# Splitting a head's query and key norm over ScalarE, VectorE and GpSimd

## What is computed

```python
def rms_norm(x, g):
    xf = x.astype(F32)
    xf = xf * lax.rsqrt(jnp.mean(xf * xf, axis=-1, keepdims=True) + EPS)
    return (xf * g.astype(F32)).astype(x.dtype)

    # in mixer_ab (layer 0)
    q = rms_norm(q.reshape(b_, t, B_KV_HEADS, B_GROUP, B_HEAD_DIM), q_g)
    k = rms_norm(k.reshape(b_, t, B_KV_HEADS, B_HEAD_DIM), k_g)
    ...
        qr = rope_2d(q, row, col)
        k_all = jnp.concatenate([rope_2d(k, row, col), ctx_k], axis=1)
    y_b = gqa_attend(qr, k_all, v_all).reshape(b_, t, B_WIDTH) * jax.nn.silu(g_b)
```

## Time and profile before

| | us |
|---|---|
| median of 3 runs (lowest, highest) | 2848.95 (2845.6, 2851.0) |
| the profiled execution, device time | 2847.76 |
| its span, first to last instruction | 2846.2 |
| PE busy | 2586.5 (91%) |
| DVE busy | 1776.5 (62%) |
| ACT busy | 867.0 (30%) |
| POOL busy | 426.9 (15%) |

### The profile page before, as it was taken

One profiled execution on the slowest core, in us unless ns is written; L12 is line 12 of the kernel. 1 busy time (PEld: TensorE's weight loads), 2 busy tenths in 40 slices (PEclk: granted clock), 3 DMA queues, 4 the chain that ended last, 5 costly groups with the idle time before them and its releaser, 6 DMA issues.

```text
span 2846.2 us, 38995 instructions
## 1 busy us (share of the span) xinstructions
PE 2586.5 (91%) x12050; PEld 2050.7 (72%) x12050; DVE 1776.5 (62%) x3260; ACT 867.0 (30%) x1767; POOL 426.9 (15%) x483
## 2 busy tenths in 40 slices
PE   4779999998888979979999999999999999988995
PEld 3458877787766858868877777777777777766884
DVE  4665777777778546766445555565656555554675
ACT  4532223232222222223223333333333333322221
POOL 0000211122221110000021212121222211001001
PEclk9789999999999989989999999999999999998998
DMA  7844544444433365553432222222222222236555
GB/s 251 294 157 148 183 135 146 158 151 161 155 127 124 131 239 190 177 192 129 155 99 91 84 67 90 91 90 88 74 90 90 92 93 90 88 112 214 181 192 213
DMA packets 167001, 400.72 MB, mean 141 GB/s; under 512 B 14984, under 2 KB 16656, under 8 KB 161616
## 3 DMA queue, kind: packets, MB, share of 16 engines
q1 hardware_dynamic: 133152, 249.08, 27.3%
q0 software_dynamic: 33712, 149.96, 15.0%
HBM read 338.17 MB, written 63.18 MB: 141 GB/s over the span
## 4 chain that ended last, share of the span: by engine, by line
PE 68%; DVE 14%; DVEq 6%; DMA 4%; issue 4%; ACT 2%; POOL 0%; SPq 0%; ACTq 0%; POOLq 0%
PE ps L533 53%; PE ps L420 5%; DVE w_lo L1072 3%; PE ps L411 3%; PE ps L429 3%; DMA w_raw<-in_w_ada_dram 2%; DVEq L1099 2%; ACT w_hi L720 1%; DVE small L954 1%; DVE work L971 1%; DMA stage<-z 1%; PE ps L512 1%; DVEq L1161 1%; PE ps L553 1%; DVE work L1181 1%
## 5 line engine op out<-in xcount | busy, mean ns | idle before, releaser
L533 PE MATMUL ps<-w_hi,hT_hi 128*128 128x512 f32 x2800 | 1163.9, 416 | 14.2 <-issue 7.5
L533 PE MATMUL ps<-w_hi,hT_lo 128*128 128x512 f32 x2800 | 1107.3, 395 | 0.0
L533 PE MATMUL ps<-w_lo,hT_hi 128*128 128x512 f32 x2800 | 1106.1, 395 | 0.0
L1072 DVE TENSOR_TENSOR w_lo<-w_raw,w_hi 128x512 fp32r<-128x512 f32 x688 | 490.2, 719 | 407.2 <-ACT w_hi L720 392.8
L533 PEld LDWEIGHTS ps<-w_hi,hT_hi 128*128 128x128 f32 x2800 | 535.1, 191 | 137.7 <-issue 37.8
L533 PEld LDWEIGHTS ps<-w_hi,hT_lo 128*128 128x128 f32 x2800 | 533.3, 190 | 118.9
L533 PEld LDWEIGHTS ps<-w_lo,hT_hi 128*128 128x128 f32 x2800 | 535.7, 191 | 91.7 <-issue 1.4
L720 ACT CAST w_hi<-w_raw 128x512 fp32r<-128x512 f32 x688 | 421.1, 620 | 506.4 <-PE ps L533 440.3
L1106 DVE SCALAR_TENSOR_TENSOR ada_sum<-w_raw,cond,ada_sum 128x512 f32<-128x512 f32 x480 | 366.8, 805 | 37.7 <-issue 10.8
L681 ACT ACTIVATE work<-ps,small 128x640 f32<-128x640 f32 (+1 forms) x192 | 139.0, 724 | 579.9 <-DVE small L957 579.8
L954 DVE TENSOR_REDUCE small<-ps 128x1 f32<-128x640 f32 (+1 forms) x200 | 143.7, 718 | 106.0 <-PE ps L420 96.4
(11 more groups left out here) (173 smaller groups left out, 2242.0 us busy)
## 6 DMA issues: line engine op xcount, KB each, us to landing
w_raw<-in_w_in_dram SPq DMA_DIRECT2D x216, 512.0 KB, 3.8
w_raw<-in_w_ada_dram SPq DMA_DIRECT2D x256, 256.0 KB, 3.0
z<-stage POOLq DMA_DIRECT2D x27, 1280.0 KB, 5.2
w_raw<-in_w_ada_dram SPq DMA_DIRECT2D x64, 512.0 KB, 5.1
w_raw<-in_w_out_dram SPq DMA_DIRECT2D x64, 512.0 KB, 4.2
work<-z POOLq DMA_DIRECT2D x72, 320.0 KB, 3.8
work<-in_x_sample_dram POOLq DMA_DIRECT2D x12, 1024.0 KB, 5.9
work<-o POOLq DMA_DIRECT2D x8, 1280.0 KB, 8.0
```

Of the source, the lines that this page charges most:

```text
L533: last = nc.tensor.matmul(ps[:, t, :], x[:, kt, t * P:(t + 1) * P], w[:, kt % RING, :], start=(kt == 0 and i == 0), stop=(kt == KT - 1 and ...
L1072: nc.vector.tensor_tensor(w_lo[:, kt % RING, :], w_raw[:, i % RAW, kt % 2, :], w_hi[:, kt % RING, :].bitcast(F32), ALU.subtract).then_inc( ...
```

## The change

Three engines share the norm of a layer 0 head, where DVE did it alone.

- **ACT**: a new `square_head` does the squares and their sums, with one `activation` of Square and `accum_out` for each of the ten 128x128 tiles of query and key. It writes the squares themselves into `weights`. The query's five stand behind the T step with r = 5 (slot 28 of pairs 0 to 3), the key's five behind the one with r = 6 (slot 43). For head 0 they stand behind k tiles 6 and 8 of chunk C_L0 + 2; the loop over two chunks there is written out for that.
- **DVE**: `norm_head` waits for `squared`, and makes the roots only, in four parts (`rsqrt_parts`) behind the same four first steps; it signals `rooted`. `before_pairs` isn't changed: the first part for head 0 stands beside k tile 4.
- **POOL**: `rotate_head` of layer 0 waits for `rooted`, and then does the four products of 128x640 with root and weight itself, with a drain behind each, ahead of the rotation.

```diff
@@ -249,7 +249,8 @@
                 s = lambda n: sem(f"{n}_{l}")
                 self.qk_in = s("qk_in")
                 self.v_in = s("v_in")
-                self.normed = s("head_normed")
+                self.squared = s("head_squared")
+                self.rooted = s("head_rooted")
                 self.roped = s("head_roped")
                 self.t_ready = s("t_ready")
                 self.t_hi = s("t_hi")
@@ -659,7 +660,22 @@
                 project_chunk(j + C_O1, j + 31, finish_at(72, j + 20, True))
 
 
-        def attention_act(act, L, h, order=None):
+        def square_head(act, h, parts):
+
+            s = S[0]
+            act.drain()
+            if 0 in parts:
+                act.wait_ge(s.qk_in, h * 48 + 48)
+                if not isinstance(h, int) or h > 0:
+                    act.wait_ge(s.rooted, h)
+            for n in parts:
+                for t in range(TT):
+                    last = nc.scalar.activation(weights[:, n, t * P:(t + 1) * P], (q_in, k_in)[n][:, t, :], ACT.Square,
+                                                accum_out=small[:, 40 + 5 * n + t:41 + 5 * n + t])
+            if 1 in parts:
+                last.then_inc(s.squared, 1)
+
+        def attention_act(act, L, h, order=None, last_head=False):
             s = S[L.n]
             NT, NS = L.n_turn, L.n_scores
 
@@ -697,6 +713,8 @@
                         nc.scalar.copy(vv[0][:, TT, :], cv_in[:, :]).then_inc(s.v_hi, 1)
                     turn(r, pieces[r])
                     r += 1
+                    if L.maps == 1 and not last_head and r in (6, 7):
+                        square_head(act, h + 1, (r - 6,))
                 elif kind == "S":
                     if n < TS * L.maps:
                         scores(n, n // L.maps, ps[:, SC:SC + 2, 0:320], 640)
@@ -806,12 +824,18 @@
                 feed_hi(0, kt)
             split_chunk(C_L0, feed_beside(0))
             evacuate(C_L0, 0)
-            with act.Fori(0, 2) as i:
-                split_chunk(i + (C_L0 + 1))
-                evacuate(i + (C_L0 + 1), i + 1)
+            split_chunk(C_L0 + 1)
+            evacuate(C_L0 + 1, 1)
+
+            def square_first(kt):
+                if kt == 6 or kt == 8:
+                    square_head(act, 0, (kt // 2 - 3,))
+
+            split_chunk(C_L0 + 2, square_first)
+            evacuate(C_L0 + 2, 2)
 
             def pair0(i, pace, evac, order=None):
-                steps = attention_act(act, L0, i, order)
+                steps = attention_act(act, L0, i, order, order is ORDER0T)
                 split_chunk(i + C_P0, stepper(steps, pace))
                 finish(steps)
                 evac(i + C_P0, i + 3)
@@ -887,28 +911,11 @@
 
             s = S[0]
             dve.drain()
-            dve.wait_ge(s.qk_in, h * 48 + 48)
-            for n, z in enumerate((q_in, k_in)):
-                if n == 1:
-                    dve.drain()
-                nc.vector.tensor_tensor(squares[0], z[:, :, :], z[:, :, :], ALU.mult)
-                dve.drain()
-                nc.vector.tensor_reduce(small[:, 40 + 5 * n:45 + 5 * n], squares[0], AX_X, ALU.add)
-                yield
-            dve.drain()
+            dve.wait_ge(s.squared, h + 1)
             nc.vector.tensor_scalar(small[:, 40:50], small[:, 40:50], 1.0 / P, EPS, ALU.mult, ALU.add)
             dve.drain()
-            rsqrt(dve, small[:, 40:50], small[:, 50:60], small[:, 30:40])
-            yield
-            for n, (z, g) in enumerate(((q_in, gq), (k_in, gk))):
-                nc.vector.tensor_tensor(z[:, :, :], z[:, :, :],
-                                        small[:, 50 + 5 * n:55 + 5 * n].unsqueeze(2).to_broadcast([P, TT, P]), ALU.mult)
-                dve.drain()
-                last = nc.vector.tensor_tensor(z[:, :, :], z[:, :, :], g[:, :].unsqueeze(1).to_broadcast([P, TT, P]),
-                                               ALU.mult)
-                if n == 0:
-                    yield
-            dve.drain().then_inc(s.normed, 1)
+            yield from rsqrt_parts(dve, small[:, 40:50], small[:, 50:60], small[:, 30:40])
+            dve.drain().then_inc(s.rooted, 1)
 
         def norm_out(dve):
 
@@ -1405,7 +1412,15 @@
 
                 s = S[L.n]
                 if L.n == 0:
-                    wait(s.normed, h + 1)
+                    wait(s.rooted, h + 1)
+                    for n, (z, g) in enumerate(((q_in, gq), (k_in, gk))):
+                        nc.gpsimd.tensor_tensor(z[:, :, :], z[:, :, :],
+                                                small[:, 50 + 5 * n:55 + 5 * n].unsqueeze(2).to_broadcast([P, TT, P]),
+                                                ALU.mult)
+                        pool.drain()
+                        nc.gpsimd.tensor_tensor(z[:, :, :], z[:, :, :],
+                                                g[:, :].unsqueeze(1).to_broadcast([P, TT, P]), ALU.mult)
+                        pool.drain()
                 else:
                     wait(s.qk_in, h * 48 + 48)
                 half = L.dk // 4
```

## The result

The changed kernel takes **2854.0 us** (median; 2846.5 to 2862.5), the kernel before in the same comparison 2845.6 (2842.6 to 2851.2). The ratio is 1.0027 with a 95% interval of 1.0017 to 1.0036: slower, by 5 to 10 us. The forecast was 2870 in a range of 2852 to 2890. The sign was right and the time lies just inside the range, but of the 21.6 us that the steps added up to, only 8 were there.

The account below looks back on a forecast made before the run. PE was taken to bound the kernel, held where it waits on other engines. Pairs 0 to 3 +4.8, pairs 4 to 6 +8.5 and head 0 +8.3 make 21.6 us on 2849.0: forecast 2870, range 2852 to 2890.

Parts of the forecast that it names:

- What bounds the kernel, and the places: PE bounds; its waits for L986 and at G steps go, new ones stand at the next pairs' first T.
- Head 0, +8.3: Near 326 us DVE waits for ACT's squares: PE stalls 5.9 us, plus 1.7 clock and 0.7 afterwards.
- ACT's squares, 0.1 us a pair: Ten squares with sums on ACT, five taking 1.8 us, delay PE by 0.1 us a pair, bound 0 to 1.
- the length of POOL's chain: From `rooted` to a pair's first T: products 8.4 us a head (2.1 each), then rotation 11.7, or 12.3 in pair 4.
- the seven transitions: Starts of pairs 1 to 7: +4.8 us for the first four and +8.5 for the last three.
- The clock: A low stretch costs 1.7 us: one lost, one added per transition in pairs 0 to 3; +5.1 in pairs 4 to 6.
- Pairs 0 to 3, forecast +4.8: Four transitions at +1.2 us net: first T +0.3, ada wait -0.8, clock +1.7; PE idles 5.3 us at the start.
- Pairs 4 to 6, forecast +8.5: Later first T from POOL's longer work, +2.6, +0.4 and +0.4 us, plus 5.1 of clock; bounds 0 and +18.
- The shared port, the second rival: POOL's longer work slows DVE's ada and w_lo, making DVE late: 2894 us, or 2886 at two thirds; chance 0.15.
- DVE's busy time: Over the whole kernel, DVE's busy time falls by some 45 us net of what contention adds.
- The third rival: Room is enough for half: products 1.6 to 1.7 us, no more low clock, head 0 costs 8; 2847 to 2854; chance 0.13.
- One more sum: POOL's products at 1.4 us each, by the skill's element count, would make the total 15 us lower.

Follow-up runs that it names:

- experiment 1: The changed kernel with head 0's squares on ACT two k tiles earlier and DVE's root parts two later: 2846.7 us, ratio 0.9998 to the kernel before.
- experiment 5: As experiment 1, with the four products left out on every engine (prices them, no usable version): 2799.2 us, ratio 0.9837 to the kernel before.
- experiment 3: The kernel before with only the four products moved to POOL, squares and one-piece root still on DVE: 2858.9 us, ratio 1.0040.
- experiment 2: As experiment 1, with the four products back on DVE and POOL doing the rotation alone: 2828.0 us, ratio 0.9939 to the kernel before.

## Why the prediction was right in sign and wrong in size

- **What bounds the kernel, and the places: right.** PE's waits for L986 and at the G steps went, and waits came at the first T of pairs 1 to 5 and at the starts of pairs 6 and 7.
- **Head 0, +8.3: right**, by the mechanism given. 5.21 us of stall for 5.9, two low stretches for one, waits of 0.50 and 0.26 behind. The profile shows +9.3, and experiment 1, which takes it away, 8.
- **ACT's squares, 0.1 us a pair: right.** No wait of PE for them is seen; five with their sums take 1.5 us where I said 1.8. (The sum had left these 0.1 us out.)
- **The failed term is the length of POOL's chain**, and with it how long PE stands still at the start of a pair. I put 8.4 us for the products and 11.7 (12.3 in pair 4) for the rotation, 20.4 and 20.9 with the T's own start. From the first product to PE's T it was 517.17 - 498.48 = 18.7 us in pair 1, and 761.59 - 743.03 = 18.6 in pair 4: 1.7 and 2.3 us shorter. In pair 1 it is the products: without the gap of 0.81 us their spacing was 1.7, not 2.1, and the gap was in the forecast already, inside the 11.7. In pair 4 1.3 us are the products and 1.0 the rotation, whose last three rows lie beside DVE's stage and not beside ada and w_lo. In experiment 1, pair 1, the T comes 506.56 - 432.02 = 74.5 us after the one before it, where the forecast said 75.7 and the kernel before had 75.4.
- **What that did to the sum.** The forecast's 13.3 us for the seven transitions are +8.2 of waits (4.8 + 2.6 + 0.4 + 0.4) and +5.1 of clock. Measured, by the windows that are cut 15 us behind the first T, are waits of -6.1 and busy time (which holds the clock) of +6.5 in the changed kernel's trace, -5.8 and +4.9 in experiment 1's: +0.4 and -0.9 in all. So the waits are 14 us off, and seven chains that are 1.7 to 2.3 us shorter account for 12 to 13 of them.
- **The clock: right in the sum, by luck.** For pairs 0 to 3 the forecast let the stretch at a start and the one lost behind L986 cancel. The starts had 12 low stretches in four for 3 before, the four behind L986 went, and PE's busy time grew by 6.3 us (4.4 in experiment 1). For pairs 5 to 7 it put +5.1. The starts had nine low stretches for five, but busy time grew by 0.2 us (0.5): one stretch went elsewhere in these pairs, and in 8.6 of the 41.0 us at the low clock PE stood still (1.6 of 30.7 before), as in this window of the changed kernel, where the clock cost nothing:

```profile
932.40:936.19 3.79, 0.00 (x0) 0.50 0.49 138
```

- **By place.** Pairs 0 to 3, forecast +4.8, took +1.9 us (+0.4 in experiment 1). PE stands for 3.2 us at a start (0.65 and 2.54), not 5.3. Pairs 4 to 6, forecast +8.5, took -1.6 (-1.3): that is the larger miss, 5 us of waits and 5 of clock.
- **The shared port, the second rival.** With waits on DVE in all seven transitions and 2886 us it didn't come. But its mechanism is what PE waits for at the starts of pairs 6 and 7, and in part of pair 5: the stage is late on DVE by 3.1, 5.7 and 5.8 us (2.0, 1.5 and 2.9 before), with POOL only 0.2 to 0.3 us behind in pairs 6 and 7. With the products off POOL these waits are 1.7, 2.7 and 2.8 (experiment 5), with them on POOL and nothing else changed 3.1, 5.8 and 5.8 (experiment 3). I had weighed it only as a delay, not as a bill: DVE's busy time fell by 21.9 us, not 45, and experiments 1, 2 and 5 show that the products on POOL take from DVE the 25 us that they save it.
- **The third rival** (room for half, head 0 costs its 8, 2847 to 2854) is where the result lies, with 2854.0, at its edge: by the ratio, on the 2849.0 from which the forecast counted, it is 2857. I gave it 0.13. Its products of 1.6 to 1.7 us were the right size without the gap; its "no more low clock" was wrong.
- **One more sum was wrong.** At 1.4 us a product in place of 2.1 the seven transitions would have been 7 x 2.8 = 19.6 us cheaper, not 15.

Most of the 6.4 us by which the traces differ more than the medians is clock too: behind the pairs the changed kernel's profiled execution has three low stretches more than the kernel before (47.8 for 42.7 us lost, without the last stretch of each), in code that is the same.
